# A hybrid decoder layer with grouped experts: the first block's first product moved between the last router products, and the third block's gather issued earlier

## The reference, cut to what matters

```python
h = layer_norm(x, ln_in_g, ln_in_b)                     # x: 2048 tokens x 1024, float32
mix = hybrid_mixer(h, w_in, pool_w, pool_scale, conv_w, conv_b, w_out)
h = layer_norm(ALPHA * h + mix, ln1_g, ln1_b)           # "h1" below
# router: probs = softmax(h @ w_router) over 16 experts in 4 groups,
#   the best group by its two best scores, in it the two best experts,
#   gate = probs of the two, divided by their sum
# every expert e: its tokens in order, padded to blocks of 128 rows
#   hid = silu(xb @ w1[e]) * (xb @ w3[e]);  y = hid @ w2[e]
ffn = sum over the two experts of gate * y              # w1, w3: 1024 x 512, w2: 512 x 1024
out = layer_norm(ALPHA * h + ffn, ln2_g, ln2_b)
```

## Time and profile before

| | us |
|---|---|
| median of 3 runs | 1366.99 |
| the profiled execution | 1367.08 |
| its span, first to last instruction | 1365.1 |
| PE busy | 1319.6 |
| DVE busy | 959.2 |
| ACT busy | 512.3 |
| POOL busy | 525.0 |

### The profile page before, as it was taken

One profiled execution on the slowest core, in us unless ns is written; L12 is line 12 of the kernel. 1 busy time (PEld: TensorE's weight loads), 2 busy tenths in 40 slices (PEclk: granted clock), 3 DMA queues, 4 the chain that ended last, 5 costly groups with the idle time before them and its releaser, 6 DMA issues.

```text
span 1365.1 us, 20423 instructions
## 1 busy us (share of the span) xinstructions
PE 1319.6 (97%) x6386; PEld 1101.9 (81%) x6387; DVE 959.2 (70%) x1353; ACT 512.3 (38%) x570; POOL 525.0 (38%) x544
## 2 busy tenths in 40 slices
PE   5999999999999999999899999999999999999994
PEld 4888888888888888887688888888888888888883
DVE  7667677697759685788588875765675677776573
ACT  2433233322443233323445543442543445433340
POOL 2001110111101110021566665756565666666564
PEclk9999999999999999999899999999999999999997
DMA  9525444463455345545767774563554555666311
GB/s 266 161 77 166 144 122 170 154 196 114 154 187 154 107 139 182 204 155 187 260 252 262 267 252 157 174 236 145 181 199 179 189 176 210 241 233 226 138 55 62
DMA packets 156522, 243.58 MB, mean 178 GB/s; under 512 B 18944, under 2 KB 84992, under 8 KB 156480
## 3 DMA queue, kind: packets, MB, share of 16 engines
q1 hardware_dynamic: 118624, 154.15, 34.8%
q0 software_dynamic: 28928, 71.74, 14.8%
q10 hardware_dynamic: 8928, 17.13, 3.7%
HBM read 211.97 MB, written 64.62 MB: 203 GB/s over the span
## 4 chain that ended last, share of the span: by engine, by line
PE 48%; issue 1%; DMA 1%; DVE 1%; POOL 1%; ACT 0%; ACTq 0%; POOLq 0%; DVEq 0%
PE acc L511 15%; PE acc L513 15%; PE acc L512 15%; PE tp L542 3%; PE aux L785 1%; DMA xg<-h_scratch,gat_now 1%; DVE ring_lo L1514 0%; DVE rrow L1526 0%; POOL orow L1778 0%; ACT ring_hi L835 0%; POOL frstd L1770 0%; DVE arow L1577 0%; DVE xt_lo L1437 0%; POOL srow L1752 0%; POOL out L1828 0%
## 5 line engine op out<-in xcount | busy, mean ns | idle before, releaser
L511 PE MATMUL acc<-ring_hi 128*128 128x512 f32 (+1 forms) x800 | 309.2, 386 | 5.1 <-DVE ring_lo L1125 5.1
L513 PE MATMUL acc<-ring_hi,ring_lo 128*128 128x512 f32 (+1 forms) x800 | 305.9, 382 | 0.0
L512 PE MATMUL acc<-ring_lo,ring_hi 128*128 128x512 f32 (+1 forms) x800 | 305.6, 382 | 0.0
L511 PE MATMUL acc<-ring_hi,xt_hi 128*128 128x512 f32 x640 | 254.7, 398 | 2.0 <-DVE xt_lo L1437 1.0
L513 PE MATMUL acc<-ring_hi,xt_lo 128*128 128x512 f32 x640 | 251.0, 392 | 0.0
L512 PE MATMUL acc<-ring_lo,xt_hi 128*128 128x512 f32 x640 | 250.4, 391 | 0.0
L1651 POOL TENSOR_TENSOR small<-small 128x1 f32<-128x1 f32 x31 | 47.4, 1529 | 361.0 <-DVE small L1096 361.0
L511 PEld LDWEIGHTS acc<-ring_hi 128*128 128x128 f32 x800 | 151.6, 190 | 33.3 <-DVE ring_lo L1125 5.7
L513 PEld LDWEIGHTS acc<-ring_hi,ring_lo 128*128 128x128 f32 x800 | 151.5, 189 | 29.1
L512 PEld LDWEIGHTS acc<-ring_lo,ring_hi 128*128 128x128 f32 x800 | 151.7, 190 | 27.6
L835 ACT CAST ring_hi<-stage_x 128x2048 fp32r<-128x2048 f32 x64 | 119.4, 1914 | 76.9 <-PE acc L513 76.4
(11 more groups left out here) (260 smaller groups left out, 1880.2 us busy)
## 6 DMA issues: line engine op xcount, KB each, us to landing
stage_x<-in_exp_w SPq DMA_DIRECT2D x64, 1024.0 KB, 7.9
stage<-in_w_in SPq DMA_DIRECT2D x64, 512.0 KB, 5.4
stage<-in_exp_w SPq DMA_DIRECT2D x32, 1024.0 KB, 6.5
stage<-in_w_out SPq DMA_DIRECT2D x32, 512.0 KB, 5.3
h_scratch<-hres POOLq DMA_DIRECT2D x16, 512.0 KB, 3.0
sum_scratch<-hres ACTq DMA_DIRECT2D x16, 512.0 KB, 2.9
hrow<-in_x POOLq DMA_DIRECT2D x12, 512.0 KB, 4.8
h_scratch<-hrow POOLq DMA_DIRECT2D x12, 512.0 KB, 3.0
```

What stands on the lines that cost most here:

```text
L511: nc.tensor.matmul(dst, w_hi, x_hi, start=start, stop=False)
L512: nc.tensor.matmul(dst, w_hi, x_lo, start=False, stop=False)
L513: return nc.tensor.matmul(dst, w_lo, x_hi, start=False, stop=stop)
```

## The change

The edits by place:

- **Start.** `g_in` and `b_in` get a semaphore each; ACT splits unit 0 ahead of tile 0's copies; PE transposes tiles 2 and 3 together, behind the v section of the first half, where tile 3's transposes stood behind the b section.
- **Groups.** The 24 matmuls of block 0's w1 product go in four groups of six into `acc[3]` (not `acc[0]`), group t ahead of `route_last(t)`. For this DVE makes `xt0_lo` before tile 3's residual, not after its normalisation. `down(0, 1)` gets a wait for the silu that reads `acc[3]`.
- **Gather of block 2.** DVE counts blocks ahead of `by_col` and works out the rows of block 2 in four small operations (`gat_2`: the third column's list if expert 0 has more than two blocks, else expert 1's first column). POOL gathers block 2 ahead of its waits for `s_plist` and `s_tab`.
- **Sums.** `index_sums(0)` comes right behind `index_rows(0)`.
- **Turn of block 1.** DVE splits one unit of the next w1 ahead of the hidden rows and the other behind `x_lo(2)`.

```diff
@@ first_units @@
-                            elif j == 1:
-                                tr_tile(0, 2 + which)
+                            elif j == 1 and which == 0:
+                                tr_tile(0, 2)
+                                tr_tile(0, 3)
@@ PE, behind chunk(LAST) @@
             h1_last(0)
             for t in range(TPC):
                 if t + 1 < TPC:
                     h1_last(t + 1)
+                if t == 0:
+                    pe.wait_ge(s_xtlo, 2)
+                    pe.wait_ge(s_res, NCH * 2 * TPC)
+                for k in (2 * t, 2 * t + 1):
+                    if k % 4 == 0:
+                        pe.wait_ge(s_elo[0], k // 4 + 1)
+                    mm = three(acc[3][:], xt0_hi[:, k, :], xt0_lo[:, k, :], *unit_cols(k // 4, k % 4 * 512, 512),
+                               k == 0, k == KT - 1)
                 route_last(t)
+            mm.then_inc(s_w1, 1)
...
             pe.sem_inc(s_w2, 1)
-            pe.wait_ge(s_xtlo, 2)
-            up(0, 0, s_w1, (xt0_hi, xt0_lo))
             ranks(LAST, True)
             up(0, 1, s_w3, (xt0_hi, xt0_lo))
             list_tiles(LAST)
             hid_tile(0, hid_0)
             pe.wait_ge(s_htlo, 1)
+            pe.wait_ge(s_silu, 1)
             down(0, 1)
@@ ACT, start @@
-            for t in range(TPC):
-                tr_hi(0, t)
-                if t < 2:
-                    split_hi(t, 32, t)
-                if t == 1:
-                    load_consts()
+            split_hi(0, 32, 0)
+            tr_hi(0, 0)
+            tr_hi(0, 1)
+            split_hi(1, 32, 1)
+            load_consts()
+            tr_hi(0, 2)
+            tr_hi(0, 3)
@@ DVE, last chunk and lists @@
-                            x_lo_0()
+                                if t == TPC - 2:
+                                    x_lo_0()
...
-            V.tensor_tensor(by_col[:, :, 0], whole[:, 0:COLS], whole[:, COLS:], ALU.min)
...
-            first_expert_lo(EU - 1)
...
+            ch.link(V.tensor_scalar(more, nblk[:, 0:1], 2.0, None, ALU.is_gt))
+            tt(step_2, whole[:, 2:3], whole[:, CAP:CAP + 1], ALU.subtract)
+            tt(step_2, step_2, more, ALU.mult)
+            V.tensor_tensor(gat_2[:], step_2, whole[:, CAP:CAP + 1], ALU.add).then_inc(s_gn, 1)
+            V.tensor_tensor(by_col[:, :, 0], whole[:, 0:COLS], whole[:, COLS:], ALU.min)
...
+            first_expert_lo(EU - 1)
@@ DVE, turn @@
                 with dve.If(ends > 0):
-                    units_lo(e_of + 1, 0)
+                    units_lo(e_of + 1, 0, (0,) if first else (0, 1))
                 hid_rows(b)
                 x_lo(b + 1)
                 with dve.If(ends > 0):
+                    if first:
+                        units_lo(e_of + 1, 0, (1,))
                     units_lo(e_of + 1, 1)
@@ POOL @@
             G.memset(srow[:], 0.0).then_inc(s_szero, 1)
+            gather_rows(2)
             pool.wait_ge(s_plist, 1)
             pool.wait_ge(s_tab, 1)
             nb = pool.value_load(nblocks[0:1, 0:1], min_val=NE + 1, max_val=NB)
             index_rows(0)
+            index_sums(0)
             index_rows(1)
             index_rows(2)
-            gather_rows(2)
-            index_sums(0)
```

More of the change, by code:

```diff
@@ L148, in build @@
         gate_0, lack = small[:, 17:18], small[:, 18:19]
+        more, step_2 = small[:, 19:20], small[:, 20:21]
+        gat_2 = nc.alloc_sbuf_tensor_at("gat_2", [P, 1], U32, offset=small_at + 4 * 32)
         gat_0 = nc.alloc_sbuf_tensor_at("gat_0", [P, 1], U32, offset=small_at + 4 * 24)
@@ L337, in build @@
         mix_v = [a[:, RING1 + 2:RING, :].rearrange("p u (k t) -> p (u k) t", t=CHUNK) for a in (ring_hi, ring_lo)]
-        s_gin = sem("ln_in_loaded")
+        s_gin = sem("ln_in_g_loaded")
+        s_bin = sem("ln_in_b_loaded")
         s_const = sem("const_loaded")
@@ L470, in _ @@
             sp.dma_start(g_in[:], bc(ln_in_g)).then_inc(s_gin, 16)
-            sp.dma_start(b_in[:], bc(ln_in_b)).then_inc(s_gin, 16)
+            sp.dma_start(b_in[:], bc(ln_in_b)).then_inc(s_bin, 16)
             for j in range(CU):
@@ L731, in route_last @@
                 mm.then_inc(s_log, 1)
-            h1_last(0)
-            for t in range(TPC):
-                if t + 1 < TPC:
-                    h1_last(t + 1)
-                route_last(t)
             def x_tile(b):
@@ L756, in up @@
                 mm.then_inc(used, 1)
+            h1_last(0)
+            for t in range(TPC):
+                if t + 1 < TPC:
+                    h1_last(t + 1)
+                if t == 0:
[6 more added lines that the diff above has]
+                               k == 0, k == KT - 1)
+                route_last(t)
+            mm.then_inc(s_w1, 1)
             def down(e_of, rows_of=None):
@@ L1019, in silu @@
                     act.wait_ge(s_hid, b)
-                nc.scalar.activation(act_a[:], acc[0][:], ACT.Silu).then_inc(s_silu, 1)
+                bank = acc[3] if isinstance(b, int) and b == 0 else acc[0]
+                nc.scalar.activation(act_a[:], bank[:], ACT.Silu).then_inc(s_silu, 1)
             def final_scale(b):
@@ L1101, in norm_rows @@
                 dve.wait_ge(s_rstd, n + 1)
+                if isinstance(n, int) and n == 0:
+                    dve.wait_ge(s_bin, 16)
                 V.scalar_tensor_tensor(out=rows, in0=rows, scalar=rstd[:], in1=b, op0=ALU.mult, op1=ALU.add).then_inc(done, 1)
@@ L1409, in _ @@
             norm_stats(hres[:, 1, :], mv_1, vareps_1)
-            dve.wait_ge(s_gin, 32)
+            dve.wait_ge(s_gin, 16)
             norm_rows(0, hres[:, 0, :], g_in[:], b_in[:], s_h)
@@ L1471, in _ @@
             hid_lo(0)
-            V.tensor_tensor(by_col[:, :, 0], whole[:, 0:COLS], whole[:, COLS:], ALU.min)
-            V.tensor_copy(by_col[:, :, 1], whole[:, 0:COLS])
-            V.tensor_copy(by_col[:, :, 2], whole[:, COLS:]).then_inc(s_plist, 1)
-            first_expert_lo(EU - 1)
             dve.wait_ge(s_tset, 2)
@@ L1486, in _ @@
             ch.link(V.tensor_scalar(nblk[:, 0:1], nblk[:, 0:1], 2.0, None, ALU.max))
+            ch.link(V.tensor_scalar(more, nblk[:, 0:1], 2.0, None, ALU.is_gt))
[3 more added lines that the diff above has]
+            V.tensor_tensor(by_col[:, :, 0], whole[:, 0:COLS], whole[:, COLS:], ALU.min)
+            V.tensor_copy(by_col[:, :, 1], whole[:, 0:COLS])
+            V.tensor_copy(by_col[:, :, 2], whole[:, COLS:]).then_inc(s_plist, 1)
+            first_expert_lo(EU - 1)
             ch.link(V.tensor_tensor_scan(end[:], row_1[:], nblk[:], 0.0, ALU.mult, ALU.add))
@@ L1509, in _, with units_lo @@
             dve.sem_inc(s_tab, 1)
-            def units_lo(ex, w):
-                for h in range(2):
+            def units_lo(ex, w, halves=(0, 1)):
+                for h in halves:
                     j = 2 * w + h
@@ L1788, in index_rows @@
                 G.tensor_copy(by_blk[:, bass.ds(b, 1), :], by_col[:, bass.ds(col, 1), :]).then_inc(s_seq, 1)
-                if not (isinstance(b, int) and b < 2):
+                if not (isinstance(b, int) and b < 3):
                     pool.wait_ge(s_gat, b * 16)
@@ L1800, in gather_rows @@
                 carry(pool, s_pool_past)
-                G.indirect_dma_start(xg[:], None, h1_dram, bass.IndirectOffsetOnAxis(ap=gat_now[:, 0:1], axis=0),
+                index = gat_2 if isinstance(b, int) and b == 2 else gat_now
+                G.indirect_dma_start(xg[:], None, h1_dram, bass.IndirectOffsetOnAxis(ap=index[:, 0:1], axis=0),
                                      bounds_check=SEQ - 1, oob_is_err=False).then_inc(s_gat, 16)
```

## The result

The changed kernel takes 1369.61 us (median of 22 runs, 1367.64 to 1371.60), the kernel before beside it 1367.22 (22 runs, 1365.65 to 1369.80): a ratio of 1.0016, 95% interval 1.0009 to 1.0022. It is slower by 0.16%: inside the 0.2% that was called no change and inside the range of the prediction, but 2.7 us above its 1366.9, and with an interval that lies wholly above 1. The profiled execution took 1370.78 us, 1.2 above the median; its span is 1368.9 and its mean granted clock 0.989. Before, these were 1367.08, 1365.1 and 0.991.

What follows compares the result with a forecast made beforehand. TensorE bounds, 1319.6 us of work in a 1365.1 us span. Terms -1.56+0.2 at the start and +6.95+1.9-3.64-0.65-1.9-1.36 = +1.3 behind the last chunk give -0.1: 1366.9 us, range 1364.5 to 1370.2.

Steps and rivals of the forecast that it cites:

- Block 3's gather came 1.36 us late: At `x_tile(3)`: the old wait for block 3's gather goes, -1.36 us, with 0 as the other end.
- the rival with a late block 3: Slower rival: clock falls in groups, low clock lasts longer, block 3's gather stays late; 1368.5 to 1371.1, chance 0.16.
- the prediction priced that at nothing: Turn of block 1 on DVE: the two halves of the w1 split around the hidden rows cost 0.
- The start: First chunk: tile 3's 1.56 us wait goes, ACT's new order costs 0.2; together -1.4 us.
- The mask wait: Ahead of the ranks: PE newly waits 6.0 us for DVE's routing mask; below 4 us would be wrong.
- the prediction's most likely case: Full clock inside the groups, a clock fall in the mask wait costing 2.2 us; forecast 1366.9, chance 0.62.
- both rivals about this place: Clock holds through the mask wait: 1365.3, chance 0.12. Clock already falls in the groups: 1.64 more, within slower's 0.16.
- The slower rival's "any two": Any two of 1.64 (groups), up to 1.2 (w3 product) and 1.36 (block 3's gather) reach the 2.7 us that decides.
- the 1.64 us that the low clock took before: Old w1 product ahead of the ranks: 7.18 us against w3's 5.54, 3.3 us of it at half speed.
- The +6.95: Groups and ranks: the lists start at 638.85 against 631.90, through the mask wait and 2.2 us of low clock.
- The second half of `down(0, 1)`: Block counts stand ahead of w2's last unit on DVE: +1.9 us; a wait outside 1 to 3 would be wrong.
- Block 2's gather: At `x_tile(2)`: -6.2 us together, from 3.64 of waiting, 0.65 at the pair of splits and 1.9 of low clock.

Runs made afterwards that it cites:

- no groups (3): Changed kernel with only the groups undone, block 0's w1 product back between the last router products and the ranks: 1369.48 us, ratio 1.0001.
- block 3's gather ahead (1): Changed kernel with block 3's index and gather issued ahead of the index of block 1's sums on POOL: 1365.43 us, ratio 0.9980.
- start only (6): Kernel before with the edits of the start alone: 1369.11 us, ratio 0.9999.
- 4: Changed kernel with the groups undone and block 3's gather ahead of block 1's sums: 1364.44 us, ratio 0.9965.
- 2: Kernel before with block 3's gather ahead of block 1's sums and nothing else: 1367.16 us, ratio 0.9997.
- best without groups: Changed kernel without groups, block 3's gather ahead, ACT's old start order, w2's last split ahead of block counts; two jobs: 1362.68 us, then 1363.02.
- experiments 5: Changed kernel with block 3's gather ahead and three w1 matmuls per group, the other twelve ahead of the ranks: 1363.21 us, ratio 0.9969.
- experiment 10: Changed kernel with block 3's gather ahead, ACT's old start order, w2's last split ahead of block counts, groups half as large: 1361.32 us, ratio 0.9957.
- experiment 7: Changed kernel with block 2's gather issued behind the three index reads again, its index still early: 1373.19 us, ratio 1.0034.
- experiment 9: Changed kernel with block 3's gather ahead, ACT's old start order, w2's last split ahead of block counts, groups whole: 1364.14 us, ratio 0.9972.
- the mended kernels: Changed kernel with block 3's gather ahead, ACT's old start order, w2's last split ahead of block counts: 1364.14 us whole groups, 1361.32 half, 1363.02 none.
- experiment 8: Changed kernel without groups, block 3's gather ahead, ACT's old start order, w2's last split ahead of block counts: 1362.68 us, ratio 0.9958; again 1363.02, ratio 0.9964.

## Why the prediction was wrong

- **The step that failed is "Block 3's gather came 1.36 us late ... The sums' index and gather go out sooner and meet fewer loads, and PE reaches `x_tile(3)` later: -1.36".** It cost 3.45 us instead: 1.86 of additional waiting, and 1.59 behind it at the lower clock. Its bounds were -1.36 and 0, and both were wrong; the rival with a late block 3 had left the 1.36 as it was. The gather stands on POOL behind `index_sums(1)`, that waits for the data of the sums' gather, and that for the tables (`s_tab`), which come behind the lists. PE's way to `x_tile(3)` comes behind the lists too, so both are to be measured from there:

| from the lists, us | PE could start `x_tile(3)` | sums' gather goes out | block 3's gather goes out | `x_tile(3)` starts |
|---|---|---|---|---|
| before | 41.00 | 20.65 | 34.61 | 42.36 |
| after | 36.52 | 18.42 | 32.26 | 39.74 |
| no groups (3) | 36.46 | 18.42 | 32.26 | 40.32 |
| block 3's gather ahead (1) | 36.32 | 18.44 | 24.03 | 36.32 |
| start only (6) | 39.81 | 20.65 | 35.10 | 42.73 |

 That PE reaches `x_tile(3)` later was no slack: the lists were later by more. By the prediction's own terms PE came 4.29 us nearer to them (5.59 against 1.30), since block 2's wait and clock fall went; measured are 4.48. To be in time the gather had to come nearer by 5.65, the 4.29 and its old 1.36. It came nearer by 2.62. The prediction had "sooner" for that and no number. The groups have no part in it: without them the distances are the same to 0.1 us, and the wait is 3.86. Experiment 1 shows that it is the place behind the sums: with this gather moved alone it goes out 8.2 us nearer to the lists, the wait is gone, and the ratio goes from 1.0016 to 0.9980.
- **A part of that lateness is DVE's.** Counted from the start of each execution, the gather goes out 2.56 us later (669.07 against 666.51). Half a microsecond comes down the chain, as far as the end of the first index copy (665.93 against 665.45). The other 2.1 are the copy L1819, 2.26 us instead of 0.18. It starts with the second of DVE's pair of splits, which runs from 663.59 to 668.08, and ends with it; before, the pair had ended at 665.40. An estimate from these rows: with a copy of 0.18 the wait would have been 3.22-2.08 = 1.1 us, late still. In the turn of block 1 the change put one more split (661.40) right ahead of this pair, and the prediction priced that at nothing. Whether that is to blame was not tried, and the kernel with the start's edits alone has a copy of 2.26 us in this place without it. So the old 1.36 was also what one execution had.
- **The start: right in sum in the trace** (-1.39 against -1.36), not seen in medians. Its parts were off: unit 0 landed 0.7 later than taken and the first product came 0.59 later, not 0.2, and 1.98 us were won behind it, not 1.56. The last chunk's transposes start at 601.98 to 603.44 in the seven profiles with these edits, at 604.64 and 604.05 in the two without, so the gain is real, while its exact agreement with the forecast is luck.
- **The mask wait: right** (6.02 us against 6.0). The clock fell 3.4 us into it, not 3.9, for 6.8 us; the lists came at +4.91 against +5.59 because the ranks were 0.3 us earlier than thought and the clock came back sooner. So it went as the prediction's most likely case, and both rivals about this place were wrong: the clock did not hold through the wait, and it did not fall in the groups. (The slower rival's "any two" of its parts holds for two of the three pairs: 1.2 and 1.36 make 2.56, less than its 2.7.)
- **What the groups replace was priced wrongly.** This error does not show in the sum, since both profiles agree with their forecasts, but it is one: the 1.64 us that the low clock took before were read as the old order's price. It is what one execution paid. From the last chunk's transposes to the ranks, PE took (us; low clock of the stretch in brackets):

| kernel, profiled execution | to the ranks | to the lists |
|---|---|---|
| before | 21.45 (3.4) | 27.26 |
| no groups: experiments 3, 4, and 2 | 23.03, 23.03, 23.03 (6.8 each) | 28.85, 28.84, 28.85 |
| start only (6); best without groups, first | 26.29; 26.33 (13.7 each) | 32.11; 32.14 |
| best without groups, second | 23.05 (6.8) | 28.86 |
| half groups: experiments 5, 10 | 23.90 (6.8), 23.09 (0 up to the wait) | 29.77, 31.60 |
| whole groups: after, experiments 1, 7, 9 | 25.87, 25.82, 25.86, 25.82 (0 up to the wait) | 33.56, 32.93, 33.70, 33.70 |

 Without groups the way to the ranks was anything from 21.5 to 26.3 us in these profiles. With whole groups it was 25.8 to 25.9 each time, and 6.8 us of low clock follow, so that the lists come 0.8 to 6.4 us later than without. The +6.95 was worked out against the shortest of these executions. This fits the runs of the mended kernels, which spread over 4.1 and 4.2 us without groups and over 2.1 with whole ones; the changed kernel itself, whose gather still waits, spreads over 4.0 in 22 runs. The net cost of whole groups is 1.0 to 1.1 us by the medians of two jobs, 1.1 to 2.0 by the ratios.
- **The second half of `down(0, 1)`: +1.07 instead of +1.9.** Its wait for w2's rest was 0.57 us, outside the 1 to 3 that the prediction had named, so this sign of being wrong came. DVE came to it sooner than was worked out: one of its writes of `by_col` (L1507 now, L1473 before) took 0.32 us, where it had taken 1.09.
- **Block 2's gather: right** (3.64 us of waiting gone, the clock full in its place, -1.78 against -1.9), but for the 0.65 us of the pair of splits: from `x_tile(2)` to the first product it is 3.26 us, as before (3.25), and the product waits 1.52 us behind the hidden rows' transposes, where 0.63 stood. In experiment 9 the same wait of 1.52 ends with no releaser ("issue"); that the beginning of the block loop on PE is exposed there is likely, but was not tried.

A rule of the Trainium skill was weighed ahead of the result ("TensorE: Matmul & The Clock Gate", Part 1, The HAM clock gate: throttled after idling, released by sustained work). Its half on idling held: the clock fell in or behind the waits of 6.02 and 3.22 us of the kernel after, and in that of 3.15 us of experiment 10; the wait of 3.06 us in experiment 7 brought none. By its letter the stretches without groups should not exist: PE was busy at 1.00 in every window of them. The measurement decides: the clock fell there without idling, each time during or right behind router products, 16 columns wide, among float32 transposes. Which of the two brings it was not tried.

## What to carry to other kernels

When an engine's order is changed, follow each DMA behind the change back through everything that the issuing engine waits for ahead of it, and ask of each whether the change itself makes that late: here a gather that nobody needed to delay stood behind a wait for another one, and moving it alone was worth 4.9 us by the ratios, 3.45 between two profiles. Measure both, the transfer and the engine that needs it, from the last point that they have in common: a change that brings the one nearer makes the other late. Put a transfer with a deadline ahead of a wait that does not concern it. And do not read the price of a low-clock stretch from one profile: take the same program's profile twice, or look at the spread of its runs, before a cure is weighed against it; of a cure that fills with idling what the clock took, half may be better than all, as it was here (1361.32 against 1364.14).

## What the runs showed of the hardware

- The granted clock falls without any idling of TensorE, in a stretch of transposes and 16-column products, and for a length that differs from execution to execution of one program: 6.8 and 13.7 us in experiment 8. In the kernel before it was 3.4. Sixteen router products take 1.85 to 1.96 us at full clock and 3.57 at the low one.
- With six products of 512 columns ahead of each set of router products the clock stayed full up to the wait in all four profiles of kernels with whole groups; with three it did in one of two. Without them it fell in all seven.
- Tiny copies on GpSimd (128x1 to 128x3) here end with VectorE's subtraction of two tiles in SBUF (128x2048, 2.28 us) if they begin within one. From 640 us on, in the traces of before, after and experiment 1, 512 copies began outside such a split and took at most 0.20 us, and 77 began within one and took at least 0.41; those of the chain to block 3's gather ended 0.04 to 0.06 us behind it, after 1.95 and 2.26 us in the kernel after. The Trainium skill ("GPSIMD Engine Reference", 1. Specifications) says that GpSimd's access to SBUF is shared with VectorE and contends with its instructions of two SBUF inputs; the trace agrees, with 2 us on the way to a gather.
